# Gates of four first keys in one run of 1 KB, and one raw buffer for the experts' U

## The reference

```
q = (xt @ wq).reshape(n_tok, 8, 2, 128)            # 8 heads, two halves
t1, i1 = top_k(s1, 16); t2, i2 = top_k(s2, 16)     # the best 16 first keys and 16 second keys
top_s, top_pos = top_k(t1[..., :, None] + t2[..., None, :], 16)
expert, gate = i1 * 128 + i2 at top_pos, softmax(top_s)
h = einsum('td,ted->te', x, u[expert])             # 128 experts of a token
y = einsum('te,ted->td', gelu(h) * gate, v[expert])
x2 = layer_norm(alpha * x1 + y, ln2_g, ln2_b)
```

## Time and profile before

| | us |
|---|---|
| median of 3 runs (2938.81 to 2943.84) | 2942.8 |
| profiled execution, its own time | 2953.03 |
| its span, first to last instruction | 2951.4 |
| gates, 968 to 1237, and the wait for the last store, 1237 to 1256 | 269 and 19 |
| experts, 1256 to the end | 1695 |

### The profile page before, as it was taken

How to read it: one execution, slowest core, us unless ns; L and a number is a source line. 1 busy time by engine, 2 the same in 40 slices (tenths; PEclk the granted TensorE clock), 3 DMA queues, 4 the chain that set the end, 5 groups by cost and what they waited for, 6 DMA issues and landing times.

```text
span 2951.4 us, 40733 instructions
## 1 busy us (share of the span) xinstructions
PE 2636.3 (89%) x14800; PEld 2018.0 (68%) x14800; DVE 2206.6 (75%) x4834; ACT 1041.8 (35%) x1771; POOL 1575.4 (53%) x1187
## 2 busy tenths in 40 slices
PE   9998798989995788646899999999999999999996
PEld 7797676778774566424667776777677777777775
DVE  5614555567999988657777787777778777789999
ACT  5413333334453898611222223222222222222222
POOL 0010010126886744356666756766676777766774
PEclk9999899999997787768999999999999999999998
DMA  4424212321112999999999999999999999999995
GB/s 146 142 70 145 94 52 80 115 73 61 55 40 69 366 368 373 347 359 389 363 388 395 405 355 391 397 393 398 384 394 375 407 401 399 401 380 337 372 376 201
DMA packets 311313, 830.36 MB, mean 281 GB/s; under 512 B 30160, under 2 KB 117648, under 8 KB 311120
## 3 DMA queue, kind: packets, MB, share of 16 engines
q0 software_dynamic: 150864, 548.60, 47.9%
q1 hardware_dynamic: 160256, 279.23, 26.7%
HBM read 769.89 MB, written 57.84 MB: 280 GB/s over the span
## 4 chain that ended last, share of the span: by engine, by line
PE 15%; DMA 13%; DVE 13%; POOL 10%; issue 6%; ACT 0%; DVEq 0%; SPq 0%; ACTq 0%; POOLq 0%
DMA e_u_row<-in_u,ids 12%; POOL hold L2225 7%; POOL e_u_row L2216 3%; DVE e_u_row L2463 3%; PE psum L2268 2%; PE psum L2301 2%; PE psum L2269 2%; PE psum L2270 2%; PE psum L2302 2%; PE psum L2303 2%; PE psum L2316 2%; DVE e_y L2453 2%; DVE e_u_row L2472 1%; DVE e_vl L2421 1%; DVE hold L2472 1%
## 5 line engine op out<-in xcount | busy, mean ns | idle before, releaser
L2216 POOL DMA_INDIRECT e_u_row<-in_u,ids x384 | 488.0, 1271 | 337.7 <-DVE ids L2463 243.1
L2463 DVE CUSTOM_DVE_ANT_0 e_u_row<-e_u_row,hold 128x1024 f32<-128x1024 f32 x384 | 467.7, 1222 | 259.4 <-DMA e_u_row<-in_u,ids 258.8
L2225 POOL DMA_INDIRECT hold<-in_v,ids x376 | 441.2, 1174 | 129.3 <-issue 109.7
L2301 PE MATMUL psum<-e_vh,e_ah 128*128 128x512 f32 x1024 | 417.9, 408 | 79.5 <-DVE e_y L2453 66.2
L2302 PE MATMUL psum<-e_vl,e_ah 128*128 128x512 f32 x1024 | 407.0, 397 | 0.0
L2303 PE MATMUL psum<-e_vh,e_al 128*128 128x512 f32 x1024 | 405.7, 396 | 0.0
L2268 PE MATMUL psum<-x1d,e_uh 128*128 128x512 f32 x928 | 366.4, 395 | 0.0
L2269 PE MATMUL psum<-x1d,e_uh 128*128 128x512 f32 x928 | 362.1, 390 | 0.0
L2270 PE MATMUL psum<-x1d,e_ul 128*128 128x512 f32 x928 | 361.3, 389 | 0.0
L2301 PEld LDWEIGHTS psum<-e_vh,e_ah 128*128 128x128 f32 x1024 | 196.8, 192 | 182.6 <-DVE e_y L2453 94.1
L2453 DVE TENSOR_TENSOR e_y<-e_y,psum 128x512 f32<-128x512 f32 x464 | 298.0, 677 | 9.5 <-PE psum L2303 9.4
(11 more groups left out here) (419 smaller groups left out, 5275.3 us busy)
## 6 DMA issues: line engine op xcount, KB each, us to landing
e_vr<-in_v SPq DMA_DIRECT2D x128, 512.0 KB, 6.5
e_ur<-in_uT SPq DMA_DIRECT2D x116, 512.0 KB, 6.7
s_G<-g_tile SPq DMA_DIRECT2D x8, 4096.0 KB, 35.9
e_g<-s_G SPq DMA_DIRECT2D x64, 512.0 KB, 8.8
ids<-in_w_ch SPq DMA_DIRECT2D x17, 512.0 KB, 4.1
s_ch<-p_out POOLq DMA_DIRECT2D x16, 512.0 KB, 3.3
hold<-in_wq SPq DMA_DIRECT2D x16, 512.0 KB, 4.4
hold<-in_v,ids POOLq DMA_INDIRECT x476, 8.6
```

Of the source, the lines that this page charges most:

```text
L2216: pool.indirect_dma_start(out=u_ring[n % U_RING][:], out_offset=None, in_=io["u"], in_offset=bass.IndirectOffsetOnAxis(ap=id_u[:, s, k:k + ...
L2225: pool.indirect_dma_start(out=v_ring[m % V_RING], out_offset=None, in_=io["v"], in_offset=bass.IndirectOffsetOnAxis(ap=id_v[:, t:t + 1], a ...
L2301: nc.tensor.matmul(acc, ah[s][j][:, r], vh[s][j][:, c], start=(first and j == 0), stop=False)
L2463: nc.vector.tensor_tensor_reduce(row, row, xs[:, s, :], 1.0, 0.0, ALU.mult, ALU.add, hs[:, s, k:k + 1]).then_inc(dotted, 1)
```

## The change

Gates of four first keys are stored together: the scratch tensor has 32 parts of 1 MB in place of 64 of 512 KB, and the run that a store writes at once is 1 KB (4 keys x 64 tokens x 4 bytes) in place of 512 B. `load_gates` reads a part for two groups at once, in every second group; `e_g` grows from 4 to 8 KB a partition. The space comes from `e_ur`, which has one buffer in place of two. So `load_u(g, 1)` waits for the split of U(g,0) and `load_u(g, 0)` for that of U(g-1,1); the hidden activations of the first 6 groups go straight into `e_a[j]`, and the norm's parameters into `e_g`. SP's order is written anew; that of the other engines stays.

```diff
-                             gt[b % 2].rearrange("p (g j) t -> p g (j t)", j=2)).then_inc(stored[b % 2], 16)
+                             gt[b % 2].rearrange("p (g j) t -> p g (j t)", j=QUAD)).then_inc(stored[b % 2], 16)
...
-        ur = [sb(f"e_ur{j}", [P, KC, P]) for j in range(2)]
+        ur = sb("e_ur", [P, KC, P])
...
-        gt = sb("e_g", [P, TD // TG, 2, TG])
+        gt = sb("e_g", [P, TD // TG, QUAD, TG])
...
-        lng, lnb = (ur[j].rearrange("p k e -> p (k e)") for j in range(2))
+        lng, lnb = (gt.rearrange("p b j t -> p (b j t)")[:, j * D:(j + 1) * D] for j in range(2))
...
                     if g < SHORT:
-                        sp.wait_ge(a_mul[j], g)
-                        sp.dma_start(ur[j].rearrange("p k e -> p (k e)")[:, 0:TD],
-                                     scr["hidden"][2 * g + j]).then_inc(u_in[j], 16)
+                        sp.wait_ge(a_lo[j], g)
+                        sp.dma_start(av[j][:], scr["hidden"][2 * g + j]).then_inc(u_in[j], 16)
                     else:
                         sp.wait_ge(a_mul[j], SHORT)
-                        sp.wait_ge(u_lo[j], g - SHORT)
-                        sp.dma_start(ur[j][:], io["uT"][2 * g + j]).then_inc(u_in[j], 16)
+                        sp.wait_ge(u_lo[1 - j], g - SHORT + j)
+                        sp.dma_start(ur[:], io["uT"][2 * g + j]).then_inc(u_in[j], 16)
-
-                def load_gates(g):
+                def load_gates(n):
                     for j in range(2):
-                        sp.wait_ge(a_mul[j], g)
-                    sp.dma_start(gt[:], scr["G"][g]).then_inc(g_in, 16)
+                        sp.wait_ge(a_mul[j], QUAD // 2 * n)
+                    sp.dma_start(gt[:], scr["G"][n]).then_inc(g_in, 16)
...
                     if SHORT < g + 1 < NG:
-                        for j in range(2):
-                            load_u(g + 1, j)
-                    load_gates(g)
+                        load_u(g + 1, 0)
+                    if g % (QUAD // 2) == 0:
+                        load_gates(g // (QUAD // 2))
                     load_v(g, 0)
                     if g + 1 <= SHORT:
-                        for j in range(2):
-                            load_u(g + 1, j)
+                        load_u(g + 1, 0)
+                    if SHORT <= g + 1 < NG:
+                        load_u(g + 1, 1)
                     load_v(g, 1)
+                    if g + 1 < SHORT:
+                        load_u(g + 1, 1)
...
                 for j, src in enumerate(("ln2_g", "ln2_b")):
                     sp.wait_ge(u_lo[j], NG - SHORT)
-                    sp.dma_start(ur[j].rearrange("p k e -> p (k e)"), io[src].partition_broadcast(P)).then_inc(u_in[j], 16)
+                    for part in range(2):
+                        sp.wait_ge(a_mul[part], NG)
+                    sp.dma_start((lng, lnb)[j], io[src].partition_broadcast(P)).then_inc(u_in[j], 16)
...
                 def weigh(g, j):
-                    dve.wait_ge(g_in, 16 * (g + 1))
+                    dve.wait_ge(g_in, 16 * (g // (QUAD // 2) + 1))
                     if g < SHORT:
                         dve.wait_ge(u_in[j], 16 * (g + 1))
-                        dve.wait_ge(a_lo[j], g)
-                        src = ur[j].rearrange("p k e -> p (k e)")[:, 0:TD]
                     else:
                         dve.wait_ge(gelu[j], g - SHORT + 1)
...
-            "G": nc.dram_tensor("s_G", (NK // 2, P, TD // TG, 2, TG), F32).ap(),
+            "G": nc.dram_tensor("s_G", (NK // QUAD, P, TD // TG, QUAD, TG), F32).ap(),
```

More of the change, by code:

```diff
@@ L38 @@
 TG = 64
+QUAD = 4
 ALPHA = 2.0 ** 0.25
@@ L2343, in split_u @@
                     act.wait_ge(h_mm[j], g - SHORT)
-                    nc.scalar.activation(uh[j][:], ur[j][:], ACT.Copy).then_inc(u_hi[j], 1)
+                    nc.scalar.activation(uh[j][:], ur[:], ACT.Copy).then_inc(u_hi[j], 1)
                 def split_v(g, j):
@@ L2416, in split_u @@
                     dve.wait_ge(u_hi[j], g - SHORT + 1)
-                    nc.vector.tensor_tensor(ul[j][:], ur[j][:], uh[j][:].bitcast(F32), ALU.subtract).then_inc(u_lo[j], 1)
+                    nc.vector.tensor_tensor(ul[j][:], ur[:], uh[j][:].bitcast(F32), ALU.subtract).then_inc(u_lo[j], 1)
                 def split_v(g, j):
@@ L2424, in weigh @@
                 def weigh(g, j):
-                    dve.wait_ge(g_in, 16 * (g + 1))
+                    dve.wait_ge(g_in, 16 * (g // (QUAD // 2) + 1))
                     if g < SHORT:
                         dve.wait_ge(u_in[j], 16 * (g + 1))
-                        dve.wait_ge(a_lo[j], g)
-                        src = ur[j].rearrange("p k e -> p (k e)")[:, 0:TD]
                     else:
                         dve.wait_ge(gelu[j], g - SHORT + 1)
-                        src = av[j][:]
-                    nc.vector.tensor_tensor(av[j].rearrange("p (b t) -> p b t", t=TG), src.rearrange("p (b t) -> p b t", t=TG),
-                                            gt[:, :, j, :], ALU.mult).then_inc(a_mul[j], 1)
+                    act = av[j].rearrange("p (b t) -> p b t", t=TG)
+                    nc.vector.tensor_tensor(act, act, gt[:, :, 2 * g % QUAD + j, :], ALU.mult).then_inc(a_mul[j], 1)
                 def split_a(g, j):
```

## The result

The changed kernel takes 2948.96 us (median of 20 runs, 2942.85 to 2954.96), the kernel before, run beside it, 2943.06 (20 runs, 2930.35 to 2948.86): ratio 1.0025, 95% interval 1.0015 to 1.0036, so 4 to 11 us slower. Forecast were 2941 us and no measurable change. Single executions of one kernel scatter by 12 to 19 us (the ranges above); the profiled execution after took 2945.86 us (span 2944.2), less than that of before, which lay 10 us over its median. One execution of the experiment with 512 KB of gates elsewhere took 3708 us, at a granted clock of 0.66, and is left out of its ratio.

What follows compares the result with a forecast made beforehand. Bounds: ScalarE and DMA while gates are built, TensorE in the experts' long stretch, VectorE in the last groups. Terms -10.5 - 1 + 5 + 4.5 = -2 us gave 2941 us, range 2927 to 2959.

Steps and rivals of the forecast that it cites:

- The store: Stage building the gates: 1 KB runs make stores cheaper and shorten waits, -10.5 us, bounds 0 and -16.
- the wait at the end: Wait for the last store of gates before the experts: DMA alone, so 1.9 us of it goes.
- Rival 3: Gates' stores get no cheaper: at 1 MB pitch a 1 KB run takes 54 ns or more; 2951 us, chance 0.07.
- The start of the experts: First expert groups: the gathered row's wait takes up the time gained on gates; -1 us (-4 to +2).
- One buffer for U: Experts: U(g+1,1) loads only after the split of U(g+1,0), delaying VectorE and TensorE; +5 us, bounds 0 and +19.
- The wait shown for group 46: Example in the experts: VectorE stands 2.1 us for the second U split, and additions to y come as much later.
- TensorE's later gaps: Long stretch: later weight-load waits on additions (35.8 us) absorb earlier delay, leaving 2 to 8 us at 2640.
- the forecast 0.2 us a group: Past group 53, more sums between VectorE's two U splits leave only 0.2 us a group of the one buffer's price.
- 1 MB of gates: Last groups: the doubled gates' load lands late in even groups, holding VectorE and TensorE; +4.5 us (0 to +10).
- the second: Rival 2, experts: U loads land in 7.1 us or more, making the single buffer cost +20; 2957 us, chance 0.16.
- the first: Rival 1: store gain comes nearly in full, -14, and the second U split is covered; 2930 us, chance 0.35.

Runs made afterwards that it cites:

- the experiment with 512 KB of gates elsewhere: Changed kernel, but gates loaded 512 KB a group in one piece from the transposed U: ratio 0.9988 to the kernel before.
- the loads from elsewhere: Changed kernel with its 1 MB of gates read from the transposed U, in 4 KB or 8 KB runs: ratios 1.0042 and 1.0034 to the kernel before.
- the moved rows: Changed kernel with products of gathered U rows shifted to odd groups, or to even groups: ratios 0.9988 and 0.9998 to the kernel before.
- the fastest one: Changed kernel with rows moved to odd groups and VectorE's second U split behind two additions up to group 52: 2931.79 us, 0.9955 to before.

## Why the prediction was wrong

**The store** (-10.5) was right. From the first store of the retrieval's codes to the experts, five profiles with 512 B runs took 290.6 to 300.0 us, mean 295.8; fifteen with 1 KB runs 282.1 to 290.7, mean 285.9: 9.9 us. The total says 10.3. Its parts were a little off. By the means over these profiles ScalarE's waits on the stores fell from 9.3 to 2.8 us (6.5, where 8.6 were forecast), its waits for TensorE's products from 12.1 to 9.9, which was not forecast, and the wait at the end from 19.6 to 19.0, where 1.9 were forecast. Rival 3, that a pitch of 1 MB takes the gain away, is out at 45.8 ns a run. The row of the Trainium skill, "DMA: Bandwidth & Descriptors", section "Latency and other measured facts", on row pitches of a large power of two speaks of the pitch from one partition's row to the next. In the scratch tensor that is 4 KB, and 8 KB after the change; 512 KB and 1 MB lie between the runs of one partition. So the prediction read the page onto another pitch, and this store does not test it.

**The start of the experts** (-1) was right in that the row's wait takes up the gates' one: in group 1 the waits of 6.35 and 3.06 us became one of 9.00 for the gathered row. Its size can't be told from nothing: from the experts' first load to group 6 ten profiles with 1 MB loads took 170.4 to 174.2 us, mean 172.4, ten with 512 KB 170.9 to 176.7, mean 173.3.

```profile
1278.05 1.22 DVE L2465 CUSTOM_DVE_ANT_0 e_u_row<-e_u_row,hold 128x1024 f32<-128x1024 f32 x1 [9.00 <-DMA e_u_row<-in_u,ids]
```

**One buffer for U** (+5) was right in size: 5.9 alone, 6.8 beside the stores. The wait shown for group 46 was right as well; in all there were fewer, 23.6 us for 35. That TensorE's later gaps take up most of it went further than forecast: with 512 KB of gates in one piece the long stretch, where 2 to 8 us were to be left, is not longer with one buffer (1227.6 and 1227.2 us) than with two (1225.3 to 1230.8). Some 2.4 us stand in the last groups (from group 53 to VectorE's last product with gates 250.1 to 252.2 us in three profiles with one buffer and 512 KB, mean 250.9; 247.4 to 251.1 in seven with two, mean 248.5), as the forecast 0.2 us a group would give. The rest of the 6 us is below what single profiles show. So the size is in part luck: it was not found in the place that gave it.

**1 MB of gates** (+4.5, bounds 0 and +10) is the step that failed, in size and in place. It was costed by VectorE's wait for the gates themselves, in the last groups, and put at nothing in the long stretch. In the last groups the term was near: the load took 10.0 us to land in the median (10.1 to 11.3 forecast), and VectorE waited 0.8 us here, 1.1 to 6.0 in the seven other profiles with 1 MB issued in this order:

```profile
DVE e_a L2436 <- DMA e_g<-s_G: 0.8, 1, 0.8
```

For the long stretch the prediction said that the wait for gathered rows takes a late load up. It does, for VectorE's own waits on gates (2.2 us in all). But the rows issued beside the 1 MB land later themselves, the additions to y stand behind them, and TensorE, which has little slack there (1208.55 of 1229 us busy), waits for the additions: 28.5 us in place of 17.2, the long stretch 1241.9 us in place of 1227.2. By the ratios the reading of 1 MB costs 10.9 us (6 to 16). That size costs is shown by the loads from elsewhere; the chain is read from the traces, and the moved rows did not confirm it.

By the ratios the steps are -10.3 for the stores, +6.8 for one buffer and +10.9 for the gates, with the start in it: +7.4, the ratio of the change (5.9 us by the medians). They are differences of one series and must add up; the one buffer alone, +5.9, is the check beside it.

The rivals: the second asked for a dearer buffer and got dearer gates instead; the first asked for 14 us from the stores and a covered split, where 10.3 and +5.9 were measured. The other terms held within their intervals; this one turned the sign.

## What to carry to other kernels

Two loads merged into one move the same bytes, but not at the same time: here, in a stretch where the DMA engines are full and the bound engine has little slack, TensorE's waits rose in the groups behind the doubled load and did not fall in the others. Cost a larger transfer also by what lands later beside it, not only by when it lands itself. When an edit's gain does not show in the total, take its other half away (here: read the gates elsewhere) before doubting the gain; test a repair in both directions, since the opposite one may help too; and find by time, not by group, when a transfer runs.

## What the hardware showed

- A 4 KB gate packet read in one piece took 163 to 164 ns, from the scratch tensor or from U; read as 4 KB runs 8 KB apart, 173 to 180 ns (mean over the times in which only that load was on its queue), and the kernel 5 us longer.
- Where the load's piece of a partition is 8 KB, it went out as packets of 8 KB, 316 ns each, and 1 MB landed in 10.0 us in the median; from two parts with 4 KB pieces it took 11.2.
- Gathered rows issued in the half group in which 1 MB loads run landed in 10.3 to 10.6 us in the mean (9.3 and 9.4 with 512 KB loads), in the half group a whole group later in 7.5 to 7.6 (8.6 and 8.7).
- From 1420 to 2630 us packets of over 600 ns were more frequent on both queues in three kernels with 1 MB loads (435 to 441 against 310 to 344), but not in the fastest one (317); why, no run here shows.
